# A two-part kernel on one core: the last residual loads queued later, two unread products left out, one residual product moved up

## The reference, cut to what matters

```python
h = h + short_conv_mixer(rmsnorm(h, norm_mix_g[0]), ...)
h = h + hier_moe(rmsnorm(h, norm_ffn_g[0]), ...)
shared = shared_kv_side(h, ...)
h = h + mla_mixer(rmsnorm(h, norm_mix_g[1]), ..., *shared)
h = h + hier_moe(rmsnorm(h, norm_ffn_g[1]), ...)
return rmsnorm(h, final_norm_g)[:, N_META:]
```

## Time and profile before

| what | value |
|---|---|
| median of 3 runs | 2759.39 us (2759.09 to 2761.17) |
| the profiled execution's own time | 2757.82 us |
| its span, first to last instruction | 2756.1 us |
| mean granted TensorE clock | 0.979 |
| PE busy | 2468.3 us (90%) |
| DVE, ACT, POOL busy | 1070.4, 542.2, 347.1 us |
| DMA | 567.11 MB, mean 206 GB/s |
| layer 0: last scatter issued, next block's first load | 1584.97, 1595.53 us |
| layer 1: last scatter issued, next block's first load | 2717.01, 2727.34 us |

### The profile page before, as it was taken

How to read it: one execution, slowest core, us unless ns; L and a number is a source line. 1 busy time by engine, 2 the same in 40 slices (tenths; PEclk the granted TensorE clock), 3 DMA queues, 4 the chain that set the end, 5 groups by cost and what they waited for, 6 DMA issues and landing times. The chain is left out here.

```text
span 2756.1 us, 39574 instructions
## 1 busy us (share of the span) xinstructions
PE 2468.3 (90%) x16337; PEld 1534.6 (56%) x16337; DVE 1070.4 (39%) x2211; ACT 542.2 (20%) x1228; POOL 347.1 (13%) x375
## 2 busy tenths in 40 slices
PE   9999988898999998987777889999999989777777
PEld 5444568547888655554444455766674555444443
DVE  3473554666455653311111154445545431111113
ACT  1312465210000011111111141322331111111112
POOL 3321102400000211111111000000003111111110
PEclk9999999999999999999999999999999999999999
DMA  3111010231013236999999980000113499999998
GB/s 118 35 38 50 23 48 5 79 115 44 33 46 119 80 127 251 422 425 425 425 425 425 398 311 21 17 24 8 56 42 138 155 402 424 424 426 425 426 424 350
DMA packets 89110, 567.11 MB, mean 206 GB/s; under 512 B 19536, under 2 KB 19696, under 8 KB 59728
## 3 DMA queue, kind: packets, MB, share of 16 engines
q1 hardware_dynamic: 63504, 506.86, 45.1%
q0 software_dynamic: 20528, 39.84, 3.8%
q10 hardware_dynamic: 4896, 17.83, 1.6%
HBM read 529.06 MB, written 66.06 MB: 216 GB/s over the span
## 5 line engine op out<-in xcount | busy, mean ns | idle before, releaser
L3267 PE MATMUL ex__h_ps<-all__arena,ex__xT 128*64 128x256 f32 x3392 | 407.1, 395 | 107.9 <-DMA all__arena<-in_w_up_t 83.8
L3267 PEld LDWEIGHTS ex__h_ps<-all__arena,ex__xT 128*64 128x64 f32 x3392 | 249.6, 142 | 277.7 <-DMA all__arena<-in_w_up_t 123.4
L3318 DVE COPY ex__ysb<-ex__y_ps 128x512 f32<-128x512 f32 x64 | 44.3, 692 | 487.1 <-PE ex__y_ps L3287 477.0
L3287 PE MATMUL ex__y_ps<-b__w,ex__hT 128*64 128x512 f32 x640 | 146.8, 600 | 26.7 <-issue 26.7
L3487 POOL DMA_INDIRECT b__rows<-s_hn,mo__queue x60 | 60.6, 1011 | 745.4 <-PE ex__x_ps L3260 745.4
L3309 DVE TENSOR_TENSOR ex__hs<-ex__sg,ex__h_ps 128x256 f32<-128x256 f32 x64 | 27.0, 422 | 304.4 <-PE ex__h_ps L3267 304.4
L2540 PE MATMUL cm__acc<-all__arena,cw__w 128*128 128x260 f32 x576 | 136.0, 386 | 2.6 <-PEq L84 2.3
L2540 PE MATMUL cm__acc<-all__arena,cm__sums 128*128 128x260 f32 x576 | 134.3, 383 | 0.0
L2540 PEld LDWEIGHTS cm__acc<-all__arena,cw__w 128*128 128x128 f32 x576 | 110.4, 192 | 20.4 <-issue 3.3
L2540 PEld LDWEIGHTS cm__acc<-all__arena,cm__sums 128*128 128x128 f32 x576 | 109.5, 190 | 17.2 <-issue 0.3
L3300 ACT COPY ex__xT<-ex__x_ps 128x512 f32<-128x512 f32 x64 | 37.5, 586 | 380.6 <-PE ex__x_ps L3260 380.6
(11 more groups left out here) (586 smaller groups left out, 4122.7 us busy)
## 6 DMA issues: line engine op xcount, KB each, us to landing
all__arena<-in_w_up_t SPq DMA_DIRECT2D x62, 2048.0 KB, 44.0
all__arena<-in_w_gate_t SPq DMA_DIRECT2D x40, 2048.0 KB, 43.5
b__w<-in_w_down_t SPq DMA_DIRECT2D x40, 2048.0 KB, 44.7
mo__wx<-in_w_gate_t SPq DMA_DIRECT2D x22, 2048.0 KB, 44.0
all__arena<-in_w_down_t SPq DMA_DIRECT2D x22, 1024.0 KB, 38.8
mo__wx<-in_w_down_t SPq DMA_DIRECT2D x20, 1024.0 KB, 44.3
all__arena<-s_ys SPq DMA_DIRECT2D x15, 1024.0 KB, 8.8
cw__w<-in_conv_w_in_t SPq DMA_DIRECT2D x24, 512.0 KB, 4.5
```

The lines of the kernel that those rows point to most:

```text
L3267: last = nc.tensor.matmul(h_ps[half, c, DE * b:DE * b + DE], xT[:, b, k, half], slots[c][:, n, k], start=(k == 0), stop=(k == KT - 1))
L3287: last = nc.tensor.matmul(y_ps[half, c], hT[:, b, k, half], rows[k][:, n, 512 * c:512 * c + 512], start=(k == 0), stop=(k == 1))
L3318: return nc.vector.tensor_copy(ysb[:, b, 512:], y_ps[:, 1])
```

## The change

It does five things:

- The last `FinalLoads` loads: in `behind_early` SP now waits for the early tiles' rows to have landed (`y_loaded`) before it issues the gain and the residuals of tiles 2 to 7.
- Behind the last scatter SP issues the rows of one tile (NE) only; the tiles up to NBUF - 1 come in the next block, at the head of its SP stream: row 2 in the latents, row 3 in the final norm.
- The residual product of each early tile but the first (tile 1 in layer 1, none in layer 0) goes ahead of the last down products, with its wait for the residual's load.
- `LatentLoads.FILL` goes from 4 to 8.
- The two unread products ahead of `turn(0)`, and their wait for `q_scaled`, are left out. `query_products(0)` waits for `q_scaled` itself.

```diff
@@ experts, SP
                 sp.wait_ge(after.last_stored, 16)
-                for t in range(NE, after.NBUF):
-                    after.rows_in(sp, t)
+                after.rows_in(sp, NE)
@@ experts, PE
+                halves = [(c, slice(512 * c, 512 * c + 512)) for c in range(2)]
+
+                def residual_product(t):
+                    pe.wait_ge(after.h_loaded[t], 16)
+                    for c, part_of in halves:
+                        nc.tensor.matmul(early_banks[t][:, c], ident[:], after.hb[:, t, part_of], start=True, stop=False)
+
+                for t in after.EARLY[1:]:
+                    residual_product(t)
                 pe.wait_ge(m["hT_out"], PAIRS_M)
                 pe.wait_ge(m["y_out"], 2 * (PAIRS_M - 1))
                 for k in range(2):
                     pe.wait_ge(d_ends[k], 16)
                     last = down_half((PAIRS_M - 1) % 2, d_slots[(PAIRS_M - 1) % RING].rows, k)
                 last.then_inc(m["y_done"], 1)
-                halves = [(c, slice(512 * c, 512 * c + 512)) for c in range(2)]
-                for t in after.EARLY:
-                    pe.wait_ge(after.h_loaded[t], 16)
-                    for c, part_of in halves:
-                        nc.tensor.matmul(early_banks[t][:, c], ident[:], after.hb[:, t, part_of], start=True, stop=False)
+                residual_product(0)
@@ LatentLoads
-    FILL = 4
+    FILL = 8
@@ combine_and_latents, SP
+                for t in range(len(pre.EARLY) + 1, NBUF):
+                    pre.rows_in(sp, t)
                 for dst, name in ((cos, "cos_tok"), (sin, "sin_tok")):
@@ combine_and_latents, PE
-                pe.wait_ge(q_scaled, KT)
-                for k in range(2):
-                    mm(aq[:, 1, 0:QR], wq[:, k, 0:P], wq[:, k], start=True, stop=True)
                 turn(0)
@@ FinalLoads.behind_early
+        for t in self.EARLY:
+            sp.wait_ge(self.y_loaded[t], 16)
         sp.dma_start(self.gb[:], self.D["final_norm_g_2"].partition_broadcast(P)).then_inc(self.g_loaded, 16)
@@ combine_out, SP
-                for t in range(NBUF, TT):
+                for t in range(len(pre.EARLY) + 1, TT):
                     sp.dma_start(yb[t], D["ys"][P * t:P * t + P]).then_inc(y_loaded[t], 16)
```

## The result

| | before | changed |
|---|---|---|
| median of 12 runs each | 2759.95 us | 2767.09 us |
| lowest, highest | 2757.76, 2763.33 us | 2761.56, 2771.38 us |
| ratio to before, with its 95% interval | | 1.0024 (1.0015 to 1.0033) |
| profiled execution's span | 2756.1 us | 2768.0 us |

The change makes the kernel slower, by 6.6 us of 2760 if the ratio is taken (4.1 to 9.1 by its interval). The two spans differ by more than that, 11.9 us; 4.0 of it is there before anything of the change runs, since the early row's load of layer 0 is issued at 1581.89 instead of 1577.88.

A forecast was written before the change was run, and what follows sets the result against it. Bound: PE, DVE, ACT, barrier and row loads behind the last experts, PE at the latents. +3.05 + 1.5 + 0 - 0.6 = about +4.0 us on 2757.82, median 1.6 above: 2763.4 us; range 2757.0 to 2767.6.

The forecast's parts named there:

- drowned scatter: Rival at the end: residual loads queued just ahead of the last scatter delay it; +8.2 in all, 2767.6 us; chance 0.13.
- last seam: From the start of the last hidden values' turn to the end of the span; predicted 4.55 us longer.
- Part 1: Behind the last experts: PE stands 3.5 us for tile 1's residual before the moved product; early sums 3.05 us late.
- Part 2: During PE's wait for tile 1's residual the clock falls, slowing work behind it: 1.5 us, bounds 0 and 2.
- Part 3: Final loads waiting for the early rows: delay costs nothing by itself; gain 0, bounds 0 to 2.6 us.
- Part 4: Row 3 issued in the final block: no difference, bounds -0.6 and +0.5 us; row 2's move in the latents hidden.
- Part 5: Start of the latents, unread products dropped and fill added: -0.6 us, range -2.0 to +2.0.
- free product: Rival at the end: tile 1's residual lands before 2707.6, so PE needn't wait; -1.6, 2757.8 us; chance 0.13.
- a clock that pays at both seams: Rival: lower clock costs 2.0 us at the end and 2.0 at the latents; +7, 2766.5 us; inside forecast's 0.70.

The follow-up runs named there:

- moved_no_wait: moved_alone, but the moved product reads the last gathered vectors instead of tile 1's residual, so PE has nothing to wait for; ratio 1.0003.
- moved_warm: moved_alone with four more unread products where PE stands for tile 1's residual; ratio 1.0009.
- moved_alone: The kernel before with one edit, tile 1's residual product ahead of the last down products; ratio 1.0011.
- in_turn: The kernel before with tile 0's residual and last-row products ahead of tile 1's, all behind the down products; ratio 1.0000.
- moved_row3: moved_alone with row 3 issued in the final block, without the wait ahead of the final residuals; ratio 1.0020.

## Why the prediction was right or wrong

The range, 2757.0 to 2767.6, held 2767.09, near its upper end; the forecast was slower but within 0.2% (+4.0 us), and it came out at +6.6, just beyond, with an interval that reaches below 0.2%. The chance that I gave to slower by over 0.2% was 0.28.

That the range held the time is partly luck. The dearest case without a drowned scatter was 2766.5; the measured 2767.09 is in the range only because the range took in the drowned scatter, 2767.6, which did not come. The kernel before was also 0.6 us slower here, 2759.95, than the 2759.39 that I had started from. The last seam grew by 6.2 us where I had 4.55: the final block came 5.5 us later and not 4.55, and the last row 15.9 us behind it and not 15.3. These two are the 1.6 us that I was short there. By its steps:

- **Part 1 was right.** I had PE resume 4.0 us behind the turn (2711.1 less 2707.1); it was 3.99. The cause is shown from both sides: without the wait the seam is as before (moved_no_wait), and the move alone makes most of it (4.7 of 6.2).
- **Part 2 was right in kind and too small.** I took 1.5 us for the clock, with 2 as the bound, from "work done in 3.4 us at half speed". It was 2.5 us at DVE's first sum (moved_warm), the largest miss of the sum. The clock fell 1.5 us after PE had stopped, within the 2.5 that I had allowed, but it was back only 6.8 us later: 4.8 us of work and not 3.4 ran at half speed, all of the moved product and the first down products.
- **Part 3 failed where it said that the delay "costs nothing by itself".** I asked whether the residuals would be there in time and not what would stand behind them in the queue: the rows did. By itself it costs 1.9 to 2.7 us. On top of the move and row 3 it adds nothing, which is due to part 1: I did foresee that for its gain but not for its cost. That the early rows were never slowed was right (9.3 and 9.4 us).
- **Part 4 was short in size and compared with the wrong thing.** "I take no difference, bounds -0.6 and +0.5": from the block's start to the last row it was 15.9 us for 15.3, +0.7. The count of one row at 4.7 and four at 2.5 held but for the last, which took 3.7. What I didn't see is that with the block moved by my own part 1, two rows queued at the landing would have been ahead of time: moved_alone has the last row 13.5 us behind the block. The change gives that up, 2.5 us on the last row and 1.7 on the seam in moved_row3.
- **Part 5 was too hopeful.** I took -0.6; the profiles show 0 to +0.6 at row 1's turn, and +0.3 at most against profiles whose scatter landed as late. The mechanism (the queries pay in place of the unread products) was the one named.
- **What bounds the kernel before was misread in one point.** I had the final block's start as the bound. The scatter's landing and the row queue come out later (moved_no_wait, in_turn). It didn't matter for the sum, since the change moved the block by over 5 us, past the other path.
- **The rivals.** The scatter did not drown: 8.4 us, landed 3.9 us ahead of the block. The free product was not free. Nearest is the case of a clock that pays at both seams, priced at +7, but it paid otherwise than I had it: 2.5 us instead of 2.0 at the end, and next to nothing instead of 2.0 at the latents; the rows gave the rest.

## What to carry to other kernels

Before a product is moved ahead of another on an in-order engine, look up when its operand lands, behind everything that is queued before it, and not when the engine used to come to it: here 3.5 us of waiting and 2.5 us of lower clock stood against 1.7 us that couldn't be had anyway. A load queue that is bound by bytes is better not made to wait: here that came back as 1.9 to 2.7 us at the end, and as nothing only where the late block hid it. And where two chains end together, price an edit once for each, and again with the other edits in place.

## What the runs showed that I had not expected

- The last scatter on POOL's queue took 5.1 and 5.4 us where the residual loads ran out during it (moved_alone, moved_row3: issued at 13.6 to 13.7, the last residual in at 18.2 to 18.5), 6.8 to 8.4 in the others, and one took 15.4 under the full weight stream. One piece of the 16 often straggles, by up to 2.5 us, and the stage waits for it.
- A wait of 3.5 us in the middle of steady work lowered the granted clock to 0.50 for 6.8 us in all four profiles that had it (changed twice, moved_alone, moved_row3), longer than the wait itself.
- The landing that PE stood for is that of the slowest of 16 pieces. In before, the pieces of tile 1's residual landed over 15.8 us: the median at 2705.7, ahead of the last turn, and the last at 2711.1. In before and in the changed kernel ten pieces were in 0.5 us behind the start of the turn, when PE comes to the moved product: it stands for the last six.
- Whole runs of one kernel spread over 4 to 10 us, more than most parts here. The medians could not separate moved_alone from moved_warm, while the seams of kernels with the same last seam, read from a local mark, repeat within 1 us.
